# Wider token groups in the input projection of a diffusion-transformer layer, in turn with channel groups

## The reference

```
h = adaln(x, norm_mix, shift, scale)              # (1280, 1024)
gq, gk, gv, gg, glr, sq, sk, sv = split(h @ w_in) # w_in is (1024, 2848)
...
x = x + g1 * (concat[gla, attention] @ w_o)
x = x + g2 * (square(relu(adaln(x) @ w_ff1)) @ w_ff2)
```

## Time and profile before

| what | value |
|---|---|
| median of 3 runs (lowest, highest) | 1649.64 us (1649.09, 1650.05) |
| the profiled execution, its own time | 1650.88 us |
| its span from first to last instruction | 1649.1 us |
| granted PE clock, mean over the span | 0.996 of full speed |
| PE busy | 1591.7 us, 97% of the span |
| POOL, DVE, ACT busy | 1023.7, 974.8, 682.9 us |
| projection: first item to last matmul | 40.97 to 389.6 us |
| DMA, mean over the span | 137 GB/s |

### The profile page before, as it was taken

One profiled execution on the slowest core, in us unless ns is written; L12 is line 12 of the kernel. 1 busy time (PEld: TensorE's weight loads), 2 busy tenths in 40 slices (PEclk: granted clock), 3 DMA queues, 4 the chain that ended last, 5 costly groups with the idle time before them and its releaser, 6 DMA issues.

```text
span 1649.1 us, 31938 instructions
## 1 busy us (share of the span) xinstructions
PE 1591.7 (97%) x11618; PEld 1392.7 (84%) x11618; DVE 974.8 (59%) x1505; ACT 682.9 (41%) x1205; POOL 1023.7 (62%) x786
## 2 busy tenths in 40 slices
PE   4999999998999999999899999999999999999998
PEld 1999778897788877788789898998979899998987
DVE  2813564774665676356866657566694545545458
ACT  2513323323454566213544444444535444444441
POOL 1711455574585799103678777687898767676673
PEclk9999999999899999999999999999999999999999
DMA  8344555749655664334743131332334132231313
GB/s 317 112 130 168 183 183 191 264 143 254 180 174 168 220 186 121 139 126 156 228 167 96 57 102 53 99 89 64 100 129 155 52 102 69 83 102 51 102 52 115
DMA packets 211450, 225.93 MB, mean 137 GB/s; under 512 B 52752, under 2 KB 171664, under 8 KB 208144
## 3 DMA queue, kind: packets, MB, share of 16 engines
q1 hardware_dynamic: 209248, 224.46, 42.7%
q10 hardware_dynamic: 2096, 0.02, 0.1%
HBM read 177.22 MB, written 47.24 MB: 136 GB/s over the span
## 4 chain that ended last, share of the span: by engine, by line
PE 44%; POOL 4%; DVE 1%; issue 1%; ACT 0%; DMA 0%; SPq 0%; DVEq 0%; ACTq 0%; POOLq 0%
PE ff_banks L3169 8%; PE ff_banks L3170 8%; PE ff_banks L3171 8%; PE ff_banks L3144 7%; PE ff_banks L3142 7%; PE ff_banks L3143 7%; POOL h_whi L2815 1%; POOL h_xop L2412 1%; POOL h_wlo L2827 1%; POOL h_whi L2822 1%; DVE ff_tmp L3016 0%; DMA ff_hb<-in_w_ff 0%; DVE ff_acc L3006 0%; DVE ff_acc L2973 0%; POOL h_wlo L2862 0%
## 5 line engine op out<-in xcount | busy, mean ns | idle before, releaser
L3142 PE MATMUL ff_banks<-h_xop,h_whi 128*128 128x320 f32 x888 | 275.2, 310 | 4.6 <-POOL h_whi L2815 2.0
L3144 PE MATMUL ff_banks<-h_xop,h_whi 128*128 128x320 f32 x888 | 274.4, 309 | 0.0
L3143 PE MATMUL ff_banks<-h_xop,h_whi 128*128 128x320 f32 x888 | 274.3, 309 | 0.0
L2973 DVE TENSOR_TENSOR ff_acc<-ff_acc,ff_banks 128x512 f32<-128x512 f32 x296 | 200.6, 681 | 100.6 <-PE ff_banks L3171 99.0
L3169 PE MATMUL ff_banks<-h_wlo 128*128 128x512 f32 x580 | 226.5, 390 | 1.6 <-DVE ff_acc L2973 0.8
L3171 PE MATMUL ff_banks<-h_wlo 128*128 128x512 f32 x580 | 225.6, 389 | 0.0
L2815 POOL TENSOR_TENSOR h_whi<-mid_raw,h_whi 128x512 fp32r<-128x512 f32 x149 | 207.4, 1408 | 1.4 <-ACT h_whi L2667 1.4
L2827 POOL TENSOR_TENSOR h_wlo<-mid_raw,h_wlo 128x320 fp32r<-128x320 f32 x128 | 116.6, 912 | 127.6 <-ACT mid_raw L2704 127.6
L3142 PEld LDWEIGHTS ff_banks<-h_xop,h_whi 128*128 128x128 f32 x888 | 166.7, 188 | 8.3 <-issue 4.0
L3143 PEld LDWEIGHTS ff_banks<-h_xop,h_whi 128*128 128x128 f32 x888 | 166.7, 188 | 1.1
L3144 PEld LDWEIGHTS ff_banks<-h_xop,h_whi 128*128 128x128 f32 x888 | 166.7, 188 | 0.0
(11 more groups left out here) (320 smaller groups left out, 3782.0 us busy)
## 6 DMA issues: line engine op xcount, KB each, us to landing
mid_raw<-in_w_ff SPq DMA_DIRECT2D x124, 512.0 KB, 4.3
mid_raw<-in_w_ada SPq DMA_DIRECT2D x18, 1024.0 KB, 7.5
early_room<-qk_by_channel SPq DMA_DIRECT2D x20, 512.0 KB, 4.1
proj<-prj_stage SPq DMA_DIRECT2D x60, 152.0 KB, 1.9
mid_raw<-in_w_in SPq DMA_DIRECT2D x6, 1216.0 KB, 7.3
early_room<-in_w_ada SPq DMA_DIRECT2D x6, 1024.0 KB, 10.9
decays<-early_room SPq DMA_DIRECT2D x8, 640.0 KB, 4.4
early_room<-decays SPq DMA_DIRECT2D x20, 256.0 KB, 2.8
```

Source lines behind the costliest of these rows:

```text
L2973: dve.tensor_tensor(acc[:, p, at], acc[:, p, at], down[n % RING], ALU.add).then_inc(added, 1)
L3142: pe.matmul(out, w_hi[:, k], x_hi[:, k], start=(k == 0), stop=False)
L3143: pe.matmul(out, w_hi[:, k], x_lo[:, k], start=False, stop=False)
L3144: mm = pe.matmul(out, w_lo[:, k], x_hi[:, k], start=False, stop=(k == KH - 1))
```

## The change: four token groups, each next to a channel group, and lists of places

The token columns become four groups (428, 428, 512, 456), and the channel columns four again but five entries with one of 256 cut in two of 128: token and channel groups alternate for the most part. There are 64 items. The even buffers are 512 columns wide, the odd ones 256. Every later group is split in two halves of its contraction rows: ACT makes both halves of `whi` one after the other, DVE makes `wlo` of the first half and POOL that of the second. The steps at which loads, splits, gates, heads and slices are due are given as lists. The gates' steps follow each other one step closer. SP waits for the stored items that a tile of heads needs.

```diff
-GROUPS = ((1936, 304), (2240, 304), (2544, 304), (0, 256), (256, 256), (512, 256), (768, 256), (1024, 304), (1328, 304), (1632, 304))
+GROUPS = ((1992, 428), (0, 256), (2420, 428), (256, 256), (1024, 512), (512, 128), (640, 128), (768, 256), (1536, 456))
 NG = len(GROUPS)
-COLS_IN = max(w for _, w in GROUPS)
+COLS_IN = [max(w for _, w in GROUPS[j::2]) for j in range(2)]
+RAW_IN = [0, KD * COLS_IN[0], KD * sum(COLS_IN)]
...
+        turn_at = {15: 0, 17: 1, 19: 2}
+        gate_at = {20: 0, 24: 1, 29: 2, 33: 3, 38: 4, 42: 5, 47: 6, 51: 7}
+        heads_at = {22: 0, 25: 1, 29: 2, 33: 3, 36: 4, 40: 5, 43: 6, 47: 7, 51: 8, 54: 9}
+        load_at = {10: 2, 16: 3, 24: 4, 32: 5, 42: 6, 43: 7, 47: 8}
+        high_at = {12: 2, 19: 3, 26: 4, 35: 5, 42: 6, 44: 7, 48: 8}
+        low_at = [{13: 2, 21: 3, 28: 4, 36: 5, 43: 6, 45: 7, 50: 8}, {13: 2, 20: 3, 27: 4, 36: 5, 43: 6, 45: 7, 49: 8}]
+        TAIL = 60
+        slices = [(2, 21), (2, 23), (3, 27), (3, 29), (3, 31), (4, 33), (4, 35), (4, 37), (4, 41), (6, 46), (7, 49), (7, 51), (7, 53), (8, 54), (8, 56), (8, 58)]
+        slice_load_at = {at: i for i, at in enumerate((17, 22, 24, 28, 30, 31, 34, 36, 38, 45, 48, 50, 52, 53, 55, 57))}
+        rows_at = {38: 1, 59: 2}
...
+        def split_until(eng, g):
+            if g == 0:
+                eng.wait_ge(first_lo_ready, 1)
+            else:
+                for half in range(2):
+                    eng.wait_ge(wlo_ready[half], g)
...
+        def low_half(eng, g, half):
+            src, hi_out, lo_out = half_of(g, half)
+            eng.wait_ge(whi_ready[half], g)
+            eng.tensor_tensor(lo_out, src, hi_out.bitcast(F32), ALU.subtract).then_inc(wlo_ready[half], 1)
...
+                    if n in load_at:
+                        g = load_at[n]
+                        split_until(sp, g - 2)
+                        if used_until[g - 2]:
+                            sp.wait_ge(ada.slice_used, KD + used_until[g - 2])
+                        load_group(sp, a, raw, g).then_inc(w_in[g % 2], 16)
...
-                    if n - 8 in gate_at:
-                        gates.sp_store(sp, gate_at[n - 8])
+                    if n - 6 in gate_at:
+                        gates.sp_store(sp, gate_at[n - 6])
...
+                def high_half(g, half):
+                    src, hi_out, lo_out = half_of(g, half)
+                    act.wait_ge(w_in[g % 2], 16 * (g // 2 + 1))
+                    if g >= 2:
+                        act.wait_ge(acc_ready, FIRST_ITEM[g - 1])
+                    act.activation(hi_out, src, ACT.Copy).then_inc(whi_ready[half], 1)
...
+                    if n in high_at:
+                        for half in range(2):
+                            high_half(high_at[n], half)
                     if n - 1 in gate_at:
                         gates.act_softplus(act, gate_at[n - 1])
...
+                    if n in low_at[1]:
+                        low_half(pool, low_at[1][n], 1)
                     if n in heads_at:
                         prep.pool(pool, heads_at[n])
...
+                    if n in low_at[0]:
+                        low_half(dve, low_at[0][n], 0)
...
+                    if n - 3 in gate_at:
+                        gates.dve_gate(dve, gate_at[n - 3])
                     if n - 4 in gate_at:
-                        gates.dve_gate(dve, gate_at[n - 4])
+                        gates.dve_scan(dve, gate_at[n - 4])
                     if n - 5 in gate_at:
-                        gates.dve_scan(dve, gate_at[n - 5])
-                    if n - 6 in gate_at:
-                        gates.dve_relative(dve, gate_at[n - 6])
+                        gates.dve_relative(dve, gate_at[n - 5])
```

More of the change, by code:

```diff
@@ L492 @@
 class Gates:
-    LO = C_LR - GROUPS[0][0]
     ROOM = T + 2 * NT * (P + 1) + NT * (P + 1) // 2
@@ L649, in project @@
         s = Space(nc, ctx, "prj")
-        whi = [s.sb(f"whi{j}", [P, KD, COLS_IN], F32R) for j in range(2)]
-        wlo = [s.sb(f"wlo{j}", [P, KD, COLS_IN], F32R) for j in range(2)]
+        whi = [s.sb(f"whi{j}", [P, KD, COLS_IN[j]], F32R) for j in range(2)]
+        wlo = [s.sb(f"wlo{j}", [P, KD, COLS_IN[j]], F32R) for j in range(2)]
         stage = s.sb("stage", [P, RING, HALF])
@@ L666, in project @@
         gates = Gates(s, keep, a, scratch, ps[:, 7], ps[:, 4:7], room)
[L669 to L680, removed]
+        turn_at = {15: 0, 17: 1, 19: 2}
[5 more added lines that the diff above has]
+        TAIL = 60
+        assert len(ITEMS) == 64 and max(gate_at) + 6 < TAIL and max(heads_at) + 4 < TAIL
+        slices = [(2, 21), (2, 23), (3, 27), (3, 29), (3, 31), (4, 33), (4, 35), (4, 37), (4, 41), (6, 46), (7, 49), (7, 51), (7, 53), (8, 54), (8, 56), (8, 58)]
+        slice_at = {at: i for i, (g, at) in enumerate(slices)}
+        slice_load_at = {at: i for i, at in enumerate((17, 22, 24, 28, 30, 31, 34, 36, 38, 45, 48, 50, 52, 53, 55, 57))}
         used_until = [sum(1 for g, at in slices if g <= f) for f in range(NG)]
@@ L683, in project @@
         BANK = ps[:, 7]
[L684 to L687, removed]
+        rows_at = {38: 1, 59: 2}
+        cols_at = {39: 1, 60: 2}
+        pick_at = {40: 1, 61: 2}
+        assert len(slices) == 2 * KD and all(FIRST_ITEM[g] <= at < FIRST_ITEM[g + 1] for g, at in slices)
         def on_act(n):
@@ L695, in staged_value, with wide, half_of @@
             return staged[on_act(n)], sum(1 for m in range(n + 1) if on_act(m) == on_act(n))
-        def split_slices(g):
-            return slice(0, GROUPS[g][1])
+        def wide(w, g):
+            return w[g % 2][:, :, 0:GROUPS[g][1]]
+        def half_of(g, half):
+            ks = slice(half * KH, (half + 1) * KH)
+            return raw_group(raw, g)[:, ks], wide(whi, g)[:, ks], wide(wlo, g)[:, ks]
+        def split_until(eng, g):
[8 more added lines that the diff above has]
+            eng.tensor_tensor(lo_out, src, hi_out.bitcast(F32), ALU.subtract).then_inc(wlo_ready[half], 1)
         def width(n):
@@ L808, in _, with first_high @@
             def _(act):
-                def split(g):
-                    j, cols = g % 2, split_slices(g)
-                    act.wait_ge(w_in[j], 16 * (g // 2 + 1))
+                def first_high():
+                    act.wait_ge(w_in[0], 16)
+                    act.activation(wide(whi, 0), raw_group(raw, 0), ACT.Copy).then_inc(first_hi_ready, 1)
+                def high_half(g, half):
+                    src, hi_out, lo_out = half_of(g, half)
+                    act.wait_ge(w_in[g % 2], 16 * (g // 2 + 1))
                     if g >= 2:
                         act.wait_ge(acc_ready, FIRST_ITEM[g - 1])
[L814 to L819, removed]
+                    act.activation(hi_out, src, ACT.Copy).then_inc(whi_ready[half], 1)
                 def evacuate(n):
@@ L907, in _ @@
                 ada.dve_silu(dve)
[L908 to L910 removed]
+                dve.wait_ge(first_hi_ready, 1)
+                dve.tensor_tensor(wide(wlo, 0), raw_group(raw, 0), wide(whi, 0).bitcast(F32), ALU.subtract).then_inc(first_lo_ready, 1)
                 for t in range(3):
@@ L3263, in build @@
             sm = Space(nc, outer, "mid")
-            raw = sm.sb("raw", [P, 2, KD, COLS_IN], side="right")
+            raw = sm.sb("raw", [P, RAW_IN[2]], side="right")
             keys = Keys(sm, a, scratch, raw)
```

87 lines of the change are left out of this document (30 added, 57 removed).

## The result

The changed kernel takes **1660.66 us** (median of 5 runs, 1658.62 to 1662.37), the kernel before 1649.09 us beside it (1645.43 to 1650.05). The ratio is **1.0075**, 95% interval 1.0063 to 1.0086: slower by about 12 us, where 1655.7 us in a range of 1645 to 1662 had been predicted. In the profiled executions the projection ends at 396.05 us instead of 389.57, +6.5 us; the prediction had +6.1 for it and nothing behind it. So the sum came out close for the stretch that it looked at, though two of its terms did not, and the other 3 to 6 us come from behind it.

What follows compares the result with a forecast made beforehand. PE was taken to bound the projection from 58 to 390 us. Terms -2.0 + 1.6 - 2.8 - 1.0 (old late slices) + 1.0 + 9.3 = +6.1 us on 1649.64 gave 1655.7 us, range 1645 to 1662.

Steps and rivals of the forecast that it cites:

- Token items: Token items of the projection: 200.4 us before, 198.3 after with wider groups, taken as -2.0 us (-1 to -3).
- Start: Projection's first items: more raw weights ahead of slices 4 to 7, +1.6 us; wider items partly filling PE's holes, -2.8.
- Steps 20 to 32: Projection, slice PE wants after item 31: its load, issued in step 30, lands late; +1.0 us (0 to +3).
- Steps 42 to 51: Projection, items 44 to 51: chain of late copies and loads delays the slice after item 51; PE loses +9.3 us.
- Rival 3: PE idles in step 51 and its clock is granted less, or slices after 53 slip: +12 or more, 1663 us; chance 0.05.
- The rest: Wider stores of token rows, tail step, wider raw buffer: 0 each; what follows the projection moves with its end.

Runs made afterwards that it cites:

- all three edits: Changed kernel with copies of items 28, 30, 44, 46 and 56 on ACT, slice of step 46 moved to 43, softplus ahead of group 8's halves: 1651.5 us.

## Why the prediction was right or wrong

- **Token items, -2.0: nearly.** 4.70 us at 428 and 5.01 at 456, against 4.66 and 4.96; the total is some 199 to 200 us, -1 to -2. Channel items of 512 came out at 5.45 us in the dense window (10.89 for two), 0.1 less than before, which gives some 1 us more.
- **Start, +1.6 and -2.8: right.** Item 0 starts 1.0 later, item 4 at 65.30 against the 65.8 of the prediction. PE is busy for 16.05 of the 18 us from 40 to 58 instead of 14.66: the holes were filled.
- **Steps 20 to 32, +1.0: mis-sized, measured 4.3.** The place and the cause were named (the slice after 31, loaded in step 30 behind head tile 1's stores, SP at 202.77), but the wait is 2.2 us, and the logits after 29, with a short wait for the slice behind them, add 0.4. Another 1.7 us the sum had not priced: the slice itself (+0.4) and item 32 (+1.3) run with the granted clock at 0.68 and 0.50.
- **Steps 42 to 51, +9.3: mechanism right, size and last wait off.** From the end of item 43 the chain reads: copy of 46 at 22.5 us (22.3 expected), group 8 issued at 23.1 (22.8) and landed after 7.7 (8.0), copy of 49 done at 41.3 (41.7), slice issued at 41.8 (42.2). The slice then landed in 5.6 us instead of 7.1, and PE got it at 47.4, not 49.3: +7.4. The wait before item 45 is 2.2 as worked out. But the slice after 51 waits only 0.5: PE had already lost its time at the slice after 46 (3.5, and 1.6 of clock in item 47). The prediction followed the chain that ends last and took PE as free of waits up to it, and so missed that an earlier slice hangs on the same late copies. The total did not suffer, since the chain that ends at the later slice already contains the earlier loss.
- **Clock.** Rival 3 had granted clock as its reason for more loss. It cost 1.7 (slice and item 32) and 1.6 us (item 47) here. The sum had no term for it.
- **The near hit is in part luck.** +6.5 us against +6.1 comes from errors that cancel: +3.3 in steps 20 to 32, -1.9 in steps 42 to 51, and some -1 in the channel items and -0.5 at the start. The median of 1660.66 us lies near the upper end of the range, which had room for the 5 us behind the projection that no term named.
- **The rest, 0: this step failed.** "What follows the projection isn't touched; I let it move with the end." From the end of the projection to the end of the span the three kernels with the order of before took 1259.5, 1254.8 and 1256.8 us (mean 1257.0), the eleven with the changed order 1255.4 to 1263.6 (mean 1260.6): 3.5 us more. In the changed kernel it is 3.2 us by the two profiles (1262.7), 11.6 - 6.5 = 5.1 us by the medians and 12.4 - 6.5 = 5.9 by the ratio.

One part of it is located. Before the merge SP waits for a store of the attention and only then loads the merge's tiles, which PE waits for. In the timelines of SP, the kernel before:

```profile
658.01 0.43 SPq L1058 DMA_DIRECT2D mix<-mix_glo_out  x1
660.40 0.81 SPq L2234 DMA_DIRECT2D mid_raw<-in_x_sample  x2
```

and the changed kernel:

```profile
665.66 0.43 SPq L1064 DMA_DIRECT2D mix<-mix_glo_out  x1
669.83 0.81 SPq L2239 DMA_DIRECT2D mid_raw<-in_x_sample  x2
```

The store lands in 2.3 us in the three kernels of the old order and in 3.9 to 4.2 in all eleven of the new one, and the stretch from the attention's last product of scores to the merge's first transposes is 1.6 to 1.8 us in the former, 2.6 to 4.6 in the latter (means 1.7 and 3.5). That is 1.7 of the 3.5 us. Why the same store lands later is open: the buffer's size and the scratch are excluded by a run, and it stays with 16 fewer loads ahead of it. The rest of the spread goes with two other things in the profiles. One is the granted clock just behind the projection. Windows of 44 us from its end: the kernel before, the changed one, the one before with the wider raw buffer, and the changed order with all three edits:

```profile
389.57:433.50 43.93, 36.14 (x415) 29.75 (x413) 29.20 (x58) 19.93 (x38) 29.38 (x34) 0.84 0.75 207
396.05:440.00 43.95, 35.20 (x406) 28.96 (x406) 29.73 (x58) 18.83 (x35) 27.70 (x32) 0.81 0.71 188
388.00:432.00 44.00, 34.90 (x469) 27.47 (x468) 31.78 (x64) 21.33 (x40) 30.71 (x35) 1.00 0.83 223
387.70:431.70 44.00, 35.64 (x480) 28.27 (x481) 32.02 (x67) 21.59 (x41) 30.86 (x35) 1.00 0.77 212
```

The two profiles with the full clock there take 1254.8 us (old order) and 1255.4 us (changed order) from the end of the projection on; the three with the most time at 1.2 GHz, 17.1 us each, take 1262.7 to 1263.6. The other thing is DVE's pair of instructions `early_mid<-mix_state_p`, here in the changed kernel and in the one with all three edits:

```profile
413.64 4.38 DVE L1396 TENSOR_TENSOR early_mid<-mix_state_p,keep_dec 64x256 f32<-64x256 f32 x2
404.21 1.29 DVE L1399 TENSOR_TENSOR early_mid<-mix_state_p,keep_dec 64x256 f32<-64x256 f32 x2
```

The stretch from the end of the projection to the transposes of the attention's queries takes 19.2 to 20.3 us in the six profiles where this pair takes 1.3 to 1.9 us, and 22.3 to 23.7 in the eight where it takes 3.5 to 4.7. The kernel before is among the eight, so the order of the change is not needed for it. An estimate: a straight line through the 14 profiles gives 0.4 us for each us at 1.2 GHz and 2.7 us for the changed order (standard error 0.6); the stretch that waits for the store has 1.7 of these. Neither thing is shown to be a cause: no run changes one of them alone, and the swapped places of the keys were not tested.

The Trainium skill (GPSIMD Engine Reference, "Specifications") has GpSimd and VectorE contend for a shared interface to SBUF. The trace agrees again: L496, 0.83 us alone, takes 2.91 beside POOL's 2.36 of L724. By the gap in the Trainium skill (TensorE: Matmul & The Clock Gate, "Back-to-back issue gap"), N/2.4 GHz plus 2.5 ns, a matmul would take 181 ns at 428 columns and 216 at 512. The trace has 9.41 us for 48 matmuls, 196 ns, and 10.89 for 48, 227 ns, so the measured paces are 5 to 8% slower.

## What to carry to other kernels

Before widening or reordering, write down for each load which engine's copy its queue waits for, and follow that engine's list: here an engine only half busy on average decided when the loads of a DMA queue went out, and 7 of 12 us came back by moving five copies to another engine. Follow every consumer of a late chain, not only the last, and allow for what the clock can take after a wait (1.6 and 1.7 us here), which is more likely the longer the wait. Judge a term of 1 to 4 us by medians of runs and several profiles, since the stretch behind the change moved by that much on its own. When a stall is repaired by moving its consumer, look where it reappears.

## What the runs showed of the hardware

- PE's granted clock can fall after short waits in a dense stream. After 3.5 us without matmuls (299.7 to 303.22) it is 0.72 on average over 303 to 309 and full again from 309. In the projections of these runs, after 58 us, it fell after all eight waits of 2.9 to 5.6 us, and after three of the twelve of 1.9 to 2.2. With the copies on ACT, behind a wait of 2.2 us that ends at 297.95, the same stretch shows 1.00:

```profile
303.00:306.00 3.00, 3.00 (x15) 2.46 (x14) 2.93 (x5) 0.00 (x0) 1.92 (x1) 1.00 1.05 389
306.00:309.00 3.00, 3.00 (x15) 2.49 (x14) 2.85 (x4) 2.65 (x2) 0.61 (x2) 1.00 1.07 437
```

- A load of 1.8 MB landed 7.7 us after its issue, against 7.1 for 1.2 MB before, and one of 2 MB after 8.1. What else is under way counts as much: group 5's 0.5 MB, 3.0 us behind a slice's load, landed after 8.2 us; slices of 1 MB that went out 2.3 and 2.6 us behind group 8's load (the runs with the slice moved, alone and with the softplus) landed after 10.6 and 10.1 us, and the one 5.0 us behind it, with the five copies on ACT, after 6.8.
- The same stretch of code, from the projection to the transposes of the queries, differs by up to 4.5 us between profiles of different versions, more than most of the terms argued about here.
